# Differential attention in a two-block transformer kernel: scores two tiles ahead, three buffers per map, and a norm's passes moved within a tile

## The chip, the cores and the metric
The kernel runs on one core of one Trainium2 chip. The metric is device time in microseconds, the median of three runs: 2166.36 us before the change (2164.78 to 2167.35).

## What is computed
The reference runs a first transformer block (rotary attention, dilated attention, gates, a ReLU-squared MLP, a gated side input) and then a second one: a SwiGLU half step, a hybrid mixer of retention and differential attention, attention over a memory of 256 rows, and another SwiGLU half step. All is float32, on 512 tokens of 1024 features. The change is in the hybrid mixer's differential attention. This is the part that matters, cut:

```
def diff_attention(q, k, v, lam):          # 4 heads, 2 maps of 64, v of 128
    sc = einsum('bqhmd,bkhmd->bhmqk', q_blk, k) * scale
    sc = sc - slopes * dist                # ALiBi, causal
    p = softmax(sc, axis=-1)
    a = p[:, :, 0] - lam * p[:, :, 1]
    return einsum('bhqk,bkhe->bqhe', a, v)
do = rms_norm(do, diff_norm) * (1.0 - lam_init)
...
kv = (mem_n @ w_kv)                        # memory attention's keys and values
k = rms_norm(kv[:, :, 0], k_norm)
```

## The kernel before
Every engine's program is written out by hand, in order, and the engines meet at semaphores. Each linear layer is a chain of units: a unit multiplies one 1024 x 128 slice of weights (eight tiles) with the activations in three passes (high x high, high x low, low x high; L274 to L276 in `unit`), into one of two PSUM banks `acc`. GpSimd (`split_unit`) splits every slice of weights in a high and a low part, two units deep; SyncE's queue loads the slices six ahead.

The differential attention (`diff_pe`, `diff_act`, `diff_dve`) has 16 tiles: 4 heads by 4 blocks of 128 queries. Tile t = 4h + qt has 128 (qt + 1) keys, so the widths go 128, 256, 384, 512 and start again. Between its tiles TensorE does the memory attention's key and value projection, one unit a tile (`mem_unit`: tiles 0 to 7 the keys, 256 wide, 8 to 15 the values). A tile's steps are:
- TensorE: `score` (L1277), two matmuls into the PSUM banks `sc[0]` and `sc[1]`, one for each map. A bank is free when VectorE has read the tile before.
- VectorE: `d_scored_dve` (L1048), for each map, adds the ALiBi table, takes the row maximum and writes the buffer `p_d[m]`.
- ScalarE: `exp` (L1319) in that buffer, with the row sum read behind it.
- VectorE: `inverse` (L1404, L1406), the reciprocals of both sums.
- ScalarE: `inv` (L1326) scales map 0; VectorE: `combine` (L1414) adds map 1 to it.
- TensorE: `turn` (L1286), qt + 1 transposes into `tp`; ScalarE: `copy_pt` (L1332) copies them out. After a head's last tile `pv` (L1293) multiplies with V into `ob`.

Nine tiles also carry one norm (`DIFF_STAT`: tiles 2 and 3 the last head's q and k, 4, 5, 8, 9 the memory keys "mk0" to "mk3", 6, 10, 14 the outputs "do0" to "do2"; "do3" comes after the last tile). Such a norm is: a square on ScalarE (`k_sq` L1350, `o_sq` L1342), a sum over partitions on TensorE into the one PSUM bank `st` (`stat_pe`, L320), which waits for the square and for `stat_v`, four passes on ScalarE (`stat_act`, L330 to L337), the read of `st` on VectorE (`stat_v_dve`, L350), which raises `stat_v`, a Newton step (L357) and the product with the gain (L1034, L1420, L1428). `hr` and `vb` are single, so one norm's passes follow the other's. The order of the norms is fixed by `STATS`.

Before the change, TensorE's tile is: scores of tile t + 1, sums of the tile's norm, the unit, `pv` of the head before, the transposes. ScalarE's is: `inv(t)`, exponentials of t + 1, the four norm passes, copies, and the square for the next tile's norm at the end. VectorE's is: `inverse(t)`, maxima of t + 1, `combine(t)`, the copy of the unit's result, the norm's passes. There are two buffers for each map, so a maximum waits for the transposes two tiles back.

Outside the tiles: `ret_high_act` (L1097) and `ret_low_dve` (L1102) split the last retention head's result; `v_copy` (L1363) copies both banks of the memory values at tiles 11 and 15; `high` (L1367) and the end of `o_norm` (L1432) split a head's output for the output projection `mix_out_pe`, which follows.

## Time and profile before

| | us |
|---|---|
| median of three runs | 2166.36 |
| range of the runs | 2164.78 to 2167.35 |
| the profiled execution's own time | 2164.66 |
| its span | 2162.8 |
| TensorE busy in it | 2102.0 |
| the stage of the change, of the span | 94.0 |

The span runs from the first to the last instruction of the profiled execution; its own time is 1.9 us longer. PE is TensorE's matmuls, PEld its weight loads, DVE VectorE, ACT ScalarE, POOL GpSimd. Rows of the timeline give start, duration, engine, line, operation and operands, how many instructions a row merges, and in brackets the idle time before it and what ended that.

### The profile page before, as it was taken

The numbers are of one execution on the slowest core, as the hardware profiler recorded it, in microseconds if no ns is written. First come the engines' busy times: TensorE is split into PE (matmuls) and PEld (weight loads), VectorE is DVE, ScalarE is ACT, GpSimd is POOL, SyncE is SP. The second block draws the span as 40 slices with busy tenths as digits, with TensorE's granted clock in tenths as the row PEclk, the third lists the DMA queues.
The fourth block names the chain that finished last, engine by engine and source line by source line (L and its number), as shares of the span: only waits on it lengthen the run. The fifth ranks groups of instructions, "written<-read, shape, count | busy, mean of one in ns | idle before, by whom it ended". The sixth has DMA issues, their size and how long they took to land.

```text
span 2162.8 us, 29025 instructions
## 1 busy us (share of the span) xinstructions
PE 2102.0 (97%) x9198; PEld 1672.5 (77%) x9198; DVE 775.2 (36%) x1242; ACT 501.8 (23%) x911; POOL 1396.4 (65%) x1372
## 2 busy tenths in 40 slices
PE   7999999999999999989999999999899999999997
PEld 5878866678888888767888887877667778888885
DVE  4123344443320122282223126344765452221024
ACT  2023243331210121141110012134652421110011
POOL 5643333367777777667777779655667357777675
PEclk8999999999999999999999999999999999999998
DMA  7311111122222223222222224222222112222221
GB/s 247 114 58 39 49 49 49 49 78 97 97 97 97 97 96 105 92 78 88 97 97 98 97 97 165 91 74 69 88 78 98 59 59 97 97 97 97 97 97 58
DMA packets 55682, 193.84 MB, mean 90 GB/s; under 512 B 6303, under 2 KB 8607, under 8 KB 55236
## 3 DMA queue, kind: packets, MB, share of 16 engines
q1 hardware_dynamic: 51500, 184.05, 25.2%
q10 hardware_dynamic: 4120, 8.95, 1.2%
q8 instruction: 41, 0.67, 0.1%
q14 instruction: 21, 0.17, 0.0%
HBM read 190.85 MB, written 5.27 MB: 91 GB/s over the span
## 4 chain that ended last, share of the span: by engine, by line
PE 90%; DVE 5%; ACT 3%; issue 1%; DMA 0%; DVEq 0%; POOL 0%; SPq 0%; ACTq 0%; POOLq 0%
PE acc L274 26%; PE acc L276 26%; PE acc L275 26%; PE st L320 2%; PE ob L669 1%; PE sc L654 1%; PE ob L482 1%; DVE ssum L398 1%; PE sc L495 1%; PE sc L1500 1%; PE sc L497 1%; PE tp L662 1%; DVE arena L1619 0%; PE tp L528 0%; PE st L617 0%
## 5 line engine op out<-in xcount | busy, mean ns | idle before, releaser
L1705 POOL TENSOR_TENSOR w_lo<-w_raw,w_hi 128x512 fp32r<-128x512 f32 x684 | 927.4, 1356 | 57.1
L1703 POOL TENSOR_SCALAR w_hi<-w_raw 128x512 fp32r<-128x512 f32 x684 | 471.1, 689 | 689.1 <-PE acc L276 657.4
L274 PE MATMUL acc<-h_hi,w_hi 128*128 128x512 f32 x1936 | 779.6, 403 | 20.1 <-DVE h_lo L1838 8.6
L276 PE MATMUL acc<-h_hi,w_lo 128*128 128x512 f32 x1936 | 756.4, 391 | 0.0
L275 PE MATMUL acc<-h_lo,w_hi 128*128 128x512 f32 x1936 | 756.1, 391 | 0.0
L274 PEld LDWEIGHTS acc<-h_hi,w_hi 128*128 128x128 f32 x1936 | 365.5, 189 | 112.1 <-issue 26.1
L275 PEld LDWEIGHTS acc<-h_lo,w_hi 128*128 128x128 f32 x1936 | 365.7, 189 | 84.7 <-issue 10.6
L276 PEld LDWEIGHTS acc<-h_hi,w_lo 128*128 128x128 f32 x1936 | 365.1, 189 | 77.3
L274 PE MATMUL acc<-hid_hi,w_hi 128*128 128x512 f32 x608 | 236.9, 390 | 0.1
L276 PE MATMUL acc<-hid_hi,w_lo 128*128 128x512 f32 x608 | 236.6, 389 | 0.0
L275 PE MATMUL acc<-hid_lo,w_hi 128*128 128x512 f32 x608 | 236.5, 389 | 0.0
L274 PEld LDWEIGHTS acc<-hid_hi,w_hi 128*128 128x128 f32 x608 | 114.1, 188 | 24.6 <-POOL w_lo L1705 0.7
L276 PEld LDWEIGHTS acc<-hid_hi,w_lo 128*128 128x128 f32 x608 | 114.1, 188 | 23.9
L275 PEld LDWEIGHTS acc<-hid_lo,w_hi 128*128 128x128 f32 x608 | 114.1, 188 | 23.5
L436 DVE TENSOR_TENSOR arena<-acc,rstd 128x512 f32<-128x512 f32 x64 | 44.1, 690 | 188.0 <-PE acc L276 187.0
L941 ACT ACTIVATE tmp<-tmp 128x512 f32<-128x512 f32 x44 | 27.8, 632 | 341.6 <-DVE tmp L950 341.6
L952 DVE TENSOR_TENSOR tmp<-acc,rstd 128x512 f32<-128x512 f32 x44 | 30.4, 691 | 200.4 <-PE acc L276 200.4
L421 DVE SCALAR_TENSOR_TENSOR x<-acc,x 128x512 f32 x24 | 16.6, 692 | 221.1 <-PE acc L276 220.7
L944 ACT CAST hid_hi<-tmp 128x512 f32 x44 | 27.3, 621 | 238.2 <-DVE tmp L955 238.2
L385 ACT ACTIVATE h_hi<-x,gain (+1 forms) x40 | 29.0, 725 | 186.0 <-DVE x L412 158.3
L398 DVE TENSOR_TENSOR ssum<-ssum,sq 128x512 f32<-128x512 f32 x64 | 68.3, 1067 | 9.1 <-ACT sq L388 8.4
L842 ACT ACTIVATE sq<-tmp 128x512 f32<-128x512 f32 x32 | 20.2, 633 | 209.9 <-DVE tmp L851 209.9
(255 smaller groups left out, 1774.4 us busy)
## 6 DMA issues: line engine op xcount, KB each, us to landing
w_raw<-in_wstream SPq DMA_DIRECT2D x342, 512.0 KB, 3.5
x<-in_xT SPq DMA_DIRECT2D x4, 512.0 KB, 6.4
bias_skew<-bias_rows ACTq DMA_DIRECT2D x4, 512.0 KB, 7.4
out_y<-x SPq DMA_DIRECT2D x8, 256.0 KB, 2.2
arena<-bias_skew ACTq DMA_DIRECT2D x4, 257.5 KB, 3.8
bias_skew<-bias_rows ACTq DMA_DIRECT2D x4, 256.0 KB, 8.0
arena<-in_memT ACTq DMA_DIRECT2D x1, 1024.0 KB, 8.4
arena<-in_decay ACTq DMA_DIRECT2D x1, 1024.0 KB, 11.8
```

The lines of the kernel that those rows point to most:

```text
L274: nc.tensor.matmul(dst, w_hi[:, slot, k, :], xh[:, k, :], start=first, stop=False)
L275: nc.tensor.matmul(dst, w_hi[:, slot, k, :], xl[:, k, :], start=False, stop=False)
L276: done = nc.tensor.matmul(dst, w_lo[:, slot, k, :], xh[:, k, :], start=False, stop=last)
L320: m = nc.tensor.matmul(st[:, 0:width], ones if lhs is None else lhs, part, start=j == 0, stop=j == len(parts) - 1)
L385: nc.scalar.activation(hi[:, n, :], x[:, n, :], ACT.Identity, scale=gain[:, GAINS[gname] + n:GAINS[gname] + n + 1] if isinstance(n, int) e ...
L398: nc.vector.tensor_tensor(ssum[:], ssum[:], sq[:, b, :], ALU.add).then_inc(h_sum, 1)
L436: nc.vector.tensor_tensor(dst, acc[n % 2][:, 0:width], rstd[:] if r is None else r, ALU.mult).then_inc(acc_read, 1)
L941: nc.scalar.activation(tmp[:, 0, :], tmp[:, 0, :], ACT.Silu).then_inc(pair_silu, 1)
L944: nc.scalar.copy(hid_hi[:, bass.ds(i, 1), :], tmp[:, 2:3, :]).then_inc(hid_hi_done, 1)
L952: nc.vector.tensor_tensor(tmp[:, 1, :], acc[1], rstd[:], ALU.mult).then_inc(acc_read, 1)
L1703: nc.gpsimd.tensor_scalar(w_hi[:, slot, ks, :], w_raw[:, raw, ks, :], 1.0, 0.0, ALU.mult, ALU.add).then_inc(w_rounded, 1)
L1705: nc.gpsimd.tensor_tensor(w_lo[:, slot, ks, :], w_raw[:, raw, ks, :], w_hi[:, slot, ks, :].bitcast(F32), ALU.subtract).then_inc(w_split, 1)
```

## The change
TensorE computes scores two tiles ahead instead of one, and issues them behind the tile's unit instead of in front of it. Each map gets a third buffer (two of the retention's decay tables, which are dead by then), and VectorE's maxima wait for the transposes and `combine` three tiles back. A norm's sums move from in front of the unit to the tile's end; ScalarE's four passes for them open the next tile, and VectorE's close it. `inv` is done one tile ahead, `combine` opens VectorE's tile. `k_sq` moves from the end of the tile before its sums into the tile of its sums, behind the exponentials and behind `o_sq`, which moves in front of `copy_pt`; `high` and the last step of `o_norm` (now `o_low`) move to the first tile of the head after next. `ret_low_dve(3)` moves in front of tile 1's maxima. No instruction is added or removed.

```diff
-        p_d = [[a2(28), a2(29)], [a2(32), a2(31)]]
+        p_d = [[a2(28), a2(29), a2(dt0)], [a2(32), a2(31), a2(dt0 + 1)]]
...
-            dve.wait_ge(turned, TILES0["diff"] + 4 * h + qt - 1)
-            dve.wait_ge(s("d_a"), counted(4 * h + qt - 1))
-            nc.vector.tensor_tensor_reduce(p_d[m][(e // 2) % 2][:, 0:w], sc[m][:, 0:w], alibi_s[:, h, SEQ - w:SEQ], 1.0,
+            dve.wait_ge(turned, TILES0["diff"] + 4 * h + qt - 2)
+            dve.wait_ge(s("d_a"), counted(4 * h + qt - 2))
+            nc.vector.tensor_tensor_reduce(p_d[m][(e // 2) % 3][:, 0:w], sc[m][:, 0:w], alibi_s[:, h, SEQ - w:SEQ], 1.0,
...
             d_v_turn_pe(pe, 3)
+            score(0, 1, 0)
+            score(0, 1, 1)
             for tile in range(4 * QT):
                 h, qt = divmod(tile, QT)
-                if tile < 4 * QT - 1:
-                    score((tile + 1) // QT, (tile + 1) % QT, 0)
-                    score((tile + 1) // QT, (tile + 1) % QT, 1)
-                if tile in DIFF_STAT:
-                    diff_stat_pe(pe, tile)
                 mem_unit(pe, tile)
+                if tile < 4 * QT - 2:
+                    score((tile + 2) // QT, (tile + 2) % QT, 0)
+                    score((tile + 2) // QT, (tile + 2) % QT, 1)
                 if h and qt == 0:
                     pv(h - 1)
                 turn(h, qt)
+                if tile in DIFF_STAT:
+                    diff_stat_pe(pe, tile)
             pv(3)
...
             ret_high_act(act, 3)
+            exp(0, 1, 0)
+            exp(0, 1, 1)
+            inv(0, 0)
             for tile in range(4 * QT):
                 h, qt = divmod(tile, QT)
-                inv(h, qt)
+                if tile - 1 in DIFF_STAT:
+                    stat_of(tile - 1)
                 if tile < 4 * QT - 1:
-                    exp((tile + 1) // QT, (tile + 1) % QT, 0)
-                    exp((tile + 1) // QT, (tile + 1) % QT, 1)
-                if tile in DIFF_STAT:
-                    stat_of(tile)
+                    inv((tile + 1) // QT, (tile + 1) % QT)
+                if tile < 4 * QT - 2:
+                    exp((tile + 2) // QT, (tile + 2) % QT, 0)
+                    exp((tile + 2) // QT, (tile + 2) % QT, 1)
+                if h and qt == 1:
+                    o_sq(h - 1)
+                if tile in DIFF_STAT and DIFF_STAT[tile][:2] == "mk":
+                    k_sq(int(DIFF_STAT[tile][2]))
                 if h and qt == 0:
                     o_copy(h - 1)
                 if tile in (11, 15):
                     v_copy((tile - 11) // 4)
                 copy_pt(h, qt)
-                if tile + 1 in DIFF_STAT and DIFF_STAT[tile + 1][:2] == "mk":
-                    k_sq(int(DIFF_STAT[tile + 1][2]))
-                if h and qt == 1:
-                    o_sq(h - 1)
-                if h and qt == 3:
-                    high(h - 1)
+                if h and qt == 0 and h > 1:
+                    high(h - 2)
             o_copy(3)
+            high(2)
...
+            ret_low_dve(dve, 3)
+            d_scored_dve(dve, 0, 1, 0)
+            d_scored_dve(dve, 0, 1, 1)
+            inverse(0, 0)
             for tile in range(4 * QT):
                 h, qt = divmod(tile, QT)
-                inverse(h, qt)
+                combine(h, qt)
                 if tile < 4 * QT - 1:
-                    d_scored_dve(dve, (tile + 1) // QT, (tile + 1) % QT, 0)
-                    d_scored_dve(dve, (tile + 1) // QT, (tile + 1) % QT, 1)
-                combine(h, qt)
-                if tile == 0:
-                    ret_low_dve(dve, 3)
+                    inverse((tile + 1) // QT, (tile + 1) % QT)
                 if tile < 8:
                     dve.wait_ge(w_used, 2 * (U0["mem_k"] + tile + 1))
                     nc.vector.tensor_copy(mem_k[:, tile, :], acc[tile % 2][:, 0:MEM]).then_inc(acc_read, 1)
-                if tile in DIFF_STAT:
-                    name, j = DIFF_STAT[tile], int(DIFF_STAT[tile][2])
+                if tile < 4 * QT - 2:
+                    d_scored_dve(dve, (tile + 2) // QT, (tile + 2) % QT, 0)
+                    d_scored_dve(dve, (tile + 2) // QT, (tile + 2) % QT, 1)
+                if h > 1 and qt == 0:
+                    o_low(h - 2)
+                if tile - 1 in DIFF_STAT:
+                    name, j = DIFF_STAT[tile - 1], int(DIFF_STAT[tile - 1][2])
                     if name[:2] == "mk":
                         k_norm(j)
                     elif name[:2] == "do":
                         stat_v_dve(dve, name, 128)
+                        o_norm(j)
...
-                if h and qt == 3:
-                    o_norm(h - 1)
+            o_low(2)
             stat_v_dve(dve, "do3", 128)
             o_norm(3)
+            o_low(3)
```

VectorE at the start of the stage, before: behind the last step of the retention (L1181) come tile 0's reciprocals, tile 1's maxima (L1048, each with its row for `mx`), tile 0's `combine` and then `ret_low`.

```order
L1181 TENSOR_TENSOR tmp<-tmp,arena 128x512
L1404 RECIPROCAL rl<-lsum 128x2
L1406 TENSOR_SCALAR rl<-rl,lam_t 128x1
L1048 ISA arena,mx<-sc,btmp 128x256
L1048 ISA mx 128x1
L1048 ISA arena,mx<-sc,btmp 128x256
L1048 ISA mx 128x1
L1414 SCALAR_TENSOR_TENSOR arena<-arena,rl 128x128
L1102 TENSOR_TENSOR h_lo<-tmp,h_hi 128x512
```

The same place with the change (line numbers of the changed kernel):

```order
L1181 TENSOR_TENSOR tmp<-tmp,arena 128x512
L1102 TENSOR_TENSOR h_lo<-tmp,h_hi 128x512
L1048 ISA arena,mx<-sc,btmp 128x256
L1048 ISA mx 128x1
L1048 ISA arena,mx<-sc,btmp 128x256
L1048 ISA mx 128x1
L1411 RECIPROCAL rl<-lsum 128x2
L1413 TENSOR_SCALAR rl<-rl,lam_t 128x1
L1421 SCALAR_TENSOR_TENSOR arena<-arena,rl 128x128
```

`ret_low` went from the end of the piece to its head; the maxima and `combine` stand behind it.

ScalarE around the norm step of tile 5, before. The square of mk1 (L1350) ends tile 4, tile 5 begins behind it.

```order
L1350 ACTIVATE tmp<-arena 128x512
L1326 ACTIVATE arena<-arena,rl 128x256
L1319 ACTIVATE arena,lsum<-arena,mx 128x384 x2
L330 ACTIVATE hr<-st,gain 128x256
L332 ACTIVATE hr<-hr 128x256
L335 ACTIVATE vb<-hr 128x256
L337 ACTIVATE hr<-hr 128x256
L1332 COPY arena<-tp 128x2x128
```

With the change, tile 5 begins with the passes of tile 4's norm and ends with the copy of its transposes (L1334):

```order
L330 ACTIVATE hr<-st,gain 128x256
L332 ACTIVATE hr<-hr 128x256
L335 ACTIVATE vb<-hr 128x256
L337 ACTIVATE hr<-hr 128x256
L1328 ACTIVATE arena<-arena,rl 128x384
L1321 ACTIVATE arena,lsum<-arena,mx 128x512 x2
L1344 ACTIVATE sq<-tmp 128x512
L1352 ACTIVATE tmp<-arena 128x512
L1334 COPY arena<-tp 128x2x128
```

The square of mk1 is now L1352, in tile 5, behind the exponentials of tile 7 (L1321) and the square of head 0's output (L1344).

TensorE at the same tile, before: the first transposes of tile 4, the scores of tile 6, the sums of mk1, then tile 5's unit.

```order
L1286 MATMUL tp<-mat_a,arena 128x128
L1277 MATMUL sc<-arena 128x384 x2
L320 MATMUL st<-tmp,mat_a 128x256 x2
L274 MATMUL acc<-mem_hi,w_hi 128x256
L275 MATMUL acc<-mem_lo,w_hi 128x256
L276 MATMUL acc<-mem_hi,w_lo 128x256
```

With the change, from the last matmul of tile 5's unit to the first of tile 6's:

```order
L276 MATMUL acc<-mem_hi,w_lo 128x256
L1277 MATMUL sc<-arena 128x512 x2
L1286 MATMUL tp<-mat_a,arena 128x128 x2
L320 MATMUL st<-tmp,mat_a 128x256 x2
L274 MATMUL acc<-mem_hi,w_hi 128x256
L275 MATMUL acc<-mem_lo,w_hi 128x256
```

The sums of mk1 moved from in front of tile 5's unit to behind it, and the scores in front of them are those of tile 7.

## Rows read from the trace of the kernel before

**Rows 1.** The page, part 1: busy us, share of the span, instructions.
```profile
PE 2102.0 (97%) x9198; PEld 1672.5 (77%) x9198; DVE 775.2 (36%) x1242; ACT 501.8 (23%) x911; POOL 1396.4 (65%) x1372
```

**Rows 2.** Window of the stage: length, busy us PE, PEld, DVE, ACT, POOL, clock.
```profile
1512.88:1606.87 93.99, 83.84 (x456) 61.38 (x455) 67.04 (x160) 64.44 (x155) 67.15 (x65) 1.00 0.26 90
```

**Rows 3.** Waits around the stage, TensorE: total us, times, longest.
```profile
PE tp L1286 <- DVE arena L1414: 5.4, 5, 1.5
...
PE st L320 <- ACT tmp L1350: 3.1, 4, 1.4
...
PE ob L1293 <- ACT arena L1332: 0.7, 1, 0.7
...
PE st L320 <- DVE vb L350: 0.4, 1, 0.4
...
PE st L320 <- ACT sq L1342: 0.3, 1, 0.3
```

**Rows 4.** Timeline of VectorE, start of the stage.
```profile
1518.51 0.42 DVE L1048 CUSTOM_DVE_ANT_0 arena<-sc,btmp 128x256 f32<-128x256 f32 x1
...
1518.86 0.42 DVE L1048 CUSTOM_DVE_ANT_0 arena<-sc,btmp 128x256 f32<-128x256 f32 x1
...
1519.24 0.35 DVE L1414 SCALAR_TENSOR_TENSOR arena<-arena,rl 128x128 f32<-128x128 f32 x1
1519.51 1.10 DVE L1102 TENSOR_TENSOR h_lo<-tmp,h_hi 128x512 fp32r<-128x512 f32 x1
```

**Rows 5.** Timeline of ScalarE, start of the stage.
```profile
1518.29 0.62 ACT L1097 CAST h_hi<-tmp 128x512 fp32r<-128x512 f32 x1 [1.39 <-DVE tmp L1181]
...
1519.12 0.49 ACT L1319 ACTIVATE arena<-arena,mx 128x256 f32<-128x256 f32 x1
```

**Rows 6.** Timeline of TensorE, tiles 0 to 5 and 11.
```profile
1519.65 0.33 PE L1286 MATMUL tp<-mat_a,arena 128*128 128x128 f32 x1 [1.46 <-DVE arena L1414]
1519.91 0.92 PE L1277 MATMUL sc<-arena 64*128 64x384 f32 x4
1520.76 0.39 PE L274 MATMUL acc<-mem_hi,w_hi 128*128 128x256 f32 x1
...
1523.74 0.38 PE L1286 MATMUL tp<-mat_a,arena 128*128 128x128 f32 x2
1524.05 1.13 PE L1277 MATMUL sc<-arena 64*128 64x512 f32 x4
1525.11 1.12 PE L320 MATMUL st<-sq,mat_b 128*128 128x512 f32 x2
...
1538.18 1.10 PE L320 MATMUL st<-tmp,mat_a 128*128 128x256 f32 x4 [1.37 <-ACT tmp L1350]
...
1541.99 2.32 PE L1293 MATMUL ob<-arena 128*128 128x512 f32 x8
...
1584.30 0.66 PE L1286 MATMUL tp<-mat_a,arena 128*128 128x128 f32 x4
...
1585.52 0.50 PE L1256 MATMUL acc<-w_hi,mem_hi 128*128 128x512 f32 x1
```

**Rows 7.** Timeline of VectorE, tile 3's maximum of the first map.
```profile
1525.21 0.69 DVE L1048 CUSTOM_DVE_ANT_0 arena<-sc,btmp 128x512 f32<-128x512 f32 x1 [0.53 <-PE sc L1277]
```

**Rows 8.** Timeline of ScalarE, passes of tiles 2, 3, 11 and 13.
```profile
1527.37 0.67 ACT L330 ACTIVATE hr<-st,gain 128x512 f32<-128x512 f32 x1
...
1537.40 0.63 ACT L1350 ACTIVATE tmp<-arena 128x512 f32<-128x512 f32 x1
...
1584.23 1.07 ACT L1363 COPY arena<-acc 128x512 f32<-128x512 f32 x2 [0.21 <-PE acc L1258]
```

**Rows 9.** Timeline of TensorE, two long waits elsewhere.
```profile
963.48 0.80 PE L274 MATMUL acc<-h_hi,w_hi 128*128 128x512 f32 x1 [3.11 <-DVE h_lo L915]
...
2149.57 1.72 PE L320 MATMUL st<-ssum,mat_a 128*128 128x512 f32 x2 [2.74 <-DVE ssum L398]
```

**Rows 10.** Window behind the first of them, columns as in rows 2.
```profile
963.00:969.00 6.00, 5.52 (x9) 3.07 (x10) 2.74 (x5) 2.05 (x3) 1.88 (x2) 0.51 0.08 11
```

More of the change, by code:

```diff
@@ L1285, in turn @@
                 for kt in range(qt + 1):
-                    m = nc.tensor.transpose(tp[e % 2][:, kt * P:(kt + 1) * P], p_d[0][e % 2][:, kt * P:(kt + 1) * P], ident)
+                    m = nc.tensor.transpose(tp[e % 2][:, kt * P:(kt + 1) * P], p_d[0][e % 3][:, kt * P:(kt + 1) * P], ident)
                 m.then_inc(turned, 1)
@@ L1317, in exp @@
                 act.wait_ge(row_max, WIDE0["diff"] + e + 1)
-                p = p_d[m][(e // 2) % 2][:, 0:w]
+                p = p_d[m][(e // 2) % 3][:, 0:w]
                 nc.scalar.activation(p, p, ACT.Exp, bias=mx[:, e % 8:e % 8 + 1], scale=-1.0,
@@ L1324, in inv @@
                 act.wait_ge(row_inv, TILES0["diff"] + e // 2 + 1)
-                p0 = p_d[0][(e // 2) % 2][:, 0:(qt + 1) * P]
+                p0 = p_d[0][(e // 2) % 3][:, 0:(qt + 1) * P]
                 nc.scalar.activation(p0, p0, ACT.Identity, scale=rl[:, e % 8:e % 8 + 1]).then_inc(s("d_p0"), 1)
@@ L1410, in combine @@
                 k, w = e % 8, (qt + 1) * P
-                p0, p1 = p_d[0][(e // 2) % 2][:, 0:w], p_d[1][(e // 2) % 2][:, 0:w]
+                p0, p1 = p_d[0][(e // 2) % 3][:, 0:w], p_d[1][(e // 2) % 3][:, 0:w]
                 dve.wait_ge(s("d_p0"), e // 2 + 1)
@@ L1430, in o_norm, with o_low @@
                 dve.sem_inc(hr_used, 1)
+            def o_low(h):
                 dve.wait_ge(s("d_hi"), h + 1)
                 nc.vector.tensor_tensor(h2_lo[:, 4 + h, :], tmp[:, 1, :], h2_hi[:, 4 + h, :].bitcast(F32), ALU.subtract).then_inc(s("d_lo"), 1)
+            ret_low_dve(dve, 3)
+            d_scored_dve(dve, 0, 1, 0)
+            d_scored_dve(dve, 0, 1, 1)
+            inverse(0, 0)
             for tile in range(4 * QT):
                 h, qt = divmod(tile, QT)
-                inverse(h, qt)
+                combine(h, qt)
                 if tile < 4 * QT - 1:
-                    d_scored_dve(dve, (tile + 1) // QT, (tile + 1) % QT, 0)
-                    d_scored_dve(dve, (tile + 1) // QT, (tile + 1) % QT, 1)
-                combine(h, qt)
-                if tile == 0:
-                    ret_low_dve(dve, 3)
+                    inverse((tile + 1) // QT, (tile + 1) % QT)
                 if tile < 8:
```

## The prediction

> **What bounds the kernel now.** I read the page first. TensorE is busy for 2102.0 of 2162.8 us and no other engine is above 65% [rows 1], so a change counts only where it moves TensorE's waits. The change touches one stage, the differential attention from its first scores to the first matmul of the output projection. The window view gives it 94.0 us, with TensorE busy for 83.8 of them at a granted clock of 1.00 [rows 2]; ten are waiting. The waits view names them [rows 3]: 5.4 us in five waits where a tile's transposes stand in front of VectorE's `combine`; 3.1 + 0.4 + 0.3 us in six where the sums of a norm stand in front of ScalarE's squares or of VectorE's read of `st` before; 0.7 us before the last product with V. Those 9.9 us are all that can be won, and 0.2% of the time, about what a measurement of this kernel can tell from no change, is 4.3 us.
>
> **How I price it.** A wait ends where the last thing it needs ends, so I follow TensorE's new order from issue to issue with the durations of the trace. M(t) is tile t's unit of the memory projection, S its two score matmuls, T its transposes. From issue to issue S and T take 0.85 and 0.26 us at 384 and 128 wide, 1.06 and 0.31 at 512 and 256 [rows 6]. Both maps of a tile run side by side, so VectorE can start only behind S: S of tile 3 starts at 1524.05, VectorE at 1525.21, or 1.16 later [rows 6, 7]. From there two maxima on VectorE and two exponentials on ScalarE fill 2.16 us, until ScalarE takes its next pass at 1527.37 [rows 7, 8]. The profile draws a matmul's end about 0.1 us into the next issue, so a wait counted from issue to issue is about 0.1 longer than in rows 3.
>
> **What goes.** With scores two tiles ahead, `inv` and `combine` of a tile are done before M(t) ends, so the waits of T at tiles 3, 6 and 10 go: 5.4 less 1.46 at tile 0 [rows 6] and less 0.26 at tile 15 is 3.7 us. The six norm waits of the old places go too, 3.8 us. With 0.1 for each of the nine, **8.4 us go**. The wait at tile 15 does not: there ScalarE still copies both banks of V (1.07 us, rows 8), then the transposes, and the product waits as before. The third buffers cost no instruction.
>
> **What comes.**
> - Start. VectorE's `ret_low(3)` now stands in front of tile 1's maxima. It needs ScalarE's cast, 1518.29 to 1518.91 [rows 5], and takes 1.10 [rows 4], to 1520.0. Two maxima of 256, 0.35 apart [rows 4], end near 1520.75; the exponentials (0.49 and their reads, rows 5) near 1521.5; only then come `inv(0)` (some 0.4) and `combine(0)` (0.35, rows 4), and T(0) at 1522.3, M(1) at 1522.55 against 1520.76 [rows 6]: **+1.8**.
> - Tiles 5 and 9. The sums of mk1 and mk3 need `k_sq`, which on ScalarE now stands behind the exponentials of tile t+2 and behind `o_sq`; those need S(t+2), which is now issued behind M(t). From the end of M(t): 1.16 + 2.16, then 0.53 for `o_sq` (a 512-wide pass hands over so long after its start: half of 1.07 for two copies) and 0.63 for `k_sq` [rows 8], and 0.15 until TensorE starts (1537.40 + 0.63 to 1538.18, rows 6, 8): 4.63. TensorE has S and T to do, 1.37. It waits 3.26 us, twice: **+6.5**.
> - Tiles 4 and 8: the same with S of 384 and no `o_sq`, about 3.6, but the product with V covers 2.2 [rows 6], S and T 1.1: 0.3 each, **+0.6**.
> - Tiles 3, 6 and 10: the sums wait for VectorE's read of `st` before them, now behind two maxima. Tile 3: 0.72 to the start, 0.69 for two maxima of 256, 0.69 for the read (as the 512-wide row of rows 7), 0.05, against 1.22 for S and T (1584.30 to 1585.52, the same widths) [rows 6]: 0.9. At tiles 6 and 10 S is 128 wide and the read 256, which makes 0.5 each. **+1.9**.
> - M(12) needs `v_copy(0)`, which stood behind exponentials already done and now stands behind those of tile 13: 0.72, 0.35 and two exponentials with reads (1.1), 0.55 for the first bank [rows 8] make 2.8 against 1.2 [rows 6]: **+1.6**.
>
> Sum: 1.8 + 6.5 + 0.6 + 1.9 + 1.6 = 12.4 against 8.4, so **4.0 us longer**. VectorE's closing passes of a norm lie beside M(t+1), which takes 2.98 (1520.76 to 1523.74, rows 6), and so do ScalarE's; they cost nothing. If M(t+1) didn't cover them the next `combine` would be late, about a microsecond a tile. `o_low(h-2)` holds VectorE for `high` at tiles 8 and 12; what it delays is the next `combine`, wanted only after a whole M. POOL and the DMA queues issue the same work in the same order.
>
> **The clock.** The trace has two waits of this length at full clock: 3.11 us ending at 963.48 and 2.74 us ending at 2149.57 [rows 9]. The granted clock after the first was 0.51 for six microseconds [rows 10], the lower of the two levels, 1.2 GHz: 0.49 x 6 = 2.9 us of work. The stage itself, with no wait above 1.46, kept 1.00 [rows 2]. The second wait was followed by a matmul that took 1.72 us [rows 9] where the same pair of 512-wide matmuls takes 1.1 [rows 6], so 0.6 us was lost before the work ended. A fall costs 0.6 to 2.9 us; I take 1.9, nearer to the longer wait, and one fall for the two waits, since both earlier ones had short bursts or a stage's end beside them and mine have a full unit ahead: **+1.9**. The Trainium skill speaks against this change here: "TensorE: Matmul & The Clock Gate", section "Why this matters for your kernels", asks for no long idle gaps between bursts of matmuls, since the gate goes back to half rate. By it both new waits would fall, and the sum would be 4.0 + 2 x 2.9 = 9.8; by the stage's own row it would be 4.0.
>
> Together 4.0 + 1.9 = 5.9. The profiled execution took 2164.66, so 2170.6 against its own time. The runs' median is 2166.36, 1.7 above it; against that the forecast is **2172.3 us**.
>
> **Rivals.**
> - No fall: +4.0, 2170.4, at the edge of what can be told. For it: TensorE's waits of this stage, up to 1.46 us, left the clock at 1.00 [rows 2, 6]. Against: rows 9 and 10. Chance 0.18.
> - Both fall: +7.8 to +9.8, 2174.2 to 2176.2. For it: the waits are 3.26 us and both waits above 2.5 had a slower matmul behind them. Chance 0.22.
> - The new waits are half as long: were the first map's scores out half way through S and its maximum and exponential under way while TensorE still works, the waits at tiles 5 and 9 would be 1.6 us each, and the sum 4.0 - 3.3 = +0.7, 2167.1. Against: VectorE's start at 1.16 [rows 6, 7] is behind the whole S. Chance 0.16, with all that lies between this and no change.
> - Faster: the squares come in time. The place is tiles 4, 5, 8 and 9: were `k_sq` ready when T ends, 7.1 of the 12.4 us would not come, and the kernel would be 3.1 us faster; with the reads of `st` in time too, 5.0, 2161.4. It decides where the stretch from S's start to `k_sq`'s end is shorter than S, T and the product, 1.37 us at tiles 5 and 9. For it: the old waits on `combine` are real, and a deeper look-ahead removes them. Against: the stretch is 4.63 us, and the order shows `k_sq` behind three passes that start after S. Chance 0.10, which also takes in milder gains.
> - The forecast, one fall: chance 0.34.
>
> **The numbers.** Range: from the faster case's mild half, 2164.5, to both falling at their full price, 2176.5; this leaves out some 0.1 below and less than 0.1 above. Slower by over 0.2% is the forecast (0.34), both falling (0.22) and a third of "no fall" (0.06): 0.62. Within 0.2%: the rest of "no fall" (0.12), the half waits (0.16), a mild gain (0.02): 0.30. Faster: 0.08.
>
> **What would show it.** Right: TensorE's waits on `combine` only at tile 0; two waits of about 3.2 us before the sums on `tmp`, released by ScalarE's square; about 1.6 us before M(12) released by V's copy; the stage about 98 us, 100 with a fall; a granted clock under 1.00 behind tile 5 or 9. Wrong: the waits at tiles 5 and 9 under 1.5 us, or the first product with V earlier than before by more than 2 us, would break the main term. A stage of 98 us and a clock of 1.00 would leave the sum and take away the fall.

## The result, and the profile after

The changed kernel takes **2173.23 us**, the median of seven runs (2169.23 to 2176.58). The kernel before, run beside it, took 2166.3 (seven runs). The ratio is 1.0041, 95% interval 1.0029 to 1.0053: slower, by 0.41% or 8.9 us as the ratio has it and by 6.9 as the two medians do. The forecast was 2172.3 and slower; the direction and the number came out, and the terms behind the number only in part.

TensorE's waits in the stage, in the form of rows 3 (waits view of the changed kernel, TensorE: total us, times, longest):

```profile
PE st L320 <- ACT tmp L1352: 7.6, 3, 3.1
PE sc L1277 <- DVE mx L1048: 2.1, 1, 2.1
PE st L320 <- DVE vb L350: 1.8, 3, 0.9
PE acc L1256 <- POOL w_lo L1720: 1.6, 1, 1.6
PE ob L1293 <- ACT arena L1334: 1.2, 1, 1.2
PE tp L1286 <- DVE arena L1421: 0.6, 1, 0.6
```

The five waits for `combine` of [rows 3], 5.4 us, have shrunk to one of 0.6 at the start. In their place stand three waits of the norm sums for ScalarE's square, 7.6 us. Ten waits of 14.9 us stand against twelve of 9.9. Where each is (timeline of the changed kernel, TensorE, every wait of the stage but the last product's):

```profile
1521.23 1.25 PE L1277 MATMUL sc<-arena 64*128 64x384 f32 x4 [2.13 <-DVE mx L1048]
1523.04 0.33 PE L1286 MATMUL tp<-mat_a,arena 128*128 128x128 f32 x1 [0.55 <-DVE arena L1421]
1538.74 1.13 PE L320 MATMUL st<-sq,mat_b 128*128 128x512 f32 x2 [0.88 <-DVE vb L350]
1554.68 2.04 PE L320 MATMUL st<-tmp,mat_a 128*128 128x256 f32 x4 [3.10 <-ACT tmp L1352]
1561.45 1.12 PE L320 MATMUL st<-sq,mat_a 128*128 128x512 f32 x2 [0.46 <-DVE vb L350]
1574.13 1.10 PE L320 MATMUL st<-tmp,mat_a 128*128 128x256 f32 x4 [1.40 <-ACT tmp L1352]
1582.53 2.05 PE L320 MATMUL st<-tmp,mat_a 128*128 128x256 f32 x4 [3.10 <-ACT tmp L1352]
1590.55 1.12 PE L320 MATMUL st<-sq,mat_a 128*128 128x512 f32 x2 [0.46 <-DVE vb L350]
1597.28 0.47 PE L1256 MATMUL acc<-w_hi,mem_hi 128*128 128x512 f32 x1 [1.62 <-POOL w_lo L1720]
```

In order: scores of tile 2 and transposes of tile 0, sums at tile 3, at tiles 5, 6, 8, 9 and 10, and tile 12's unit. Two of these rows show more than a wait: the sums at tiles 5 and 9 take 2.04 and 2.05 where the same row takes 1.10 at tile 8. The granted clock had fallen. The windows view shows it, first for the stage, here counted from the sums of the retention's last norm to the first matmul of the last product, then for the six microseconds behind the waits at the start and at tiles 5, 8 and 9 (columns as in rows 2):

```profile
1512.83:1616.15 103.32, 88.26 (x449) 64.77 (x448) 59.43 (x159) 63.49 (x154) 64.06 (x64) 0.93 0.24 79
1521.23:1527.23 6.00, 5.45 (x27) 4.78 (x28) 3.28 (x15) 3.94 (x12) 2.69 (x4) 0.72 0.26 90
1554.68:1560.68 6.00, 6.00 (x34) 5.39 (x35) 1.27 (x5) 2.45 (x6) 1.77 (x2) 0.74 0.16 63
1574.13:1580.13 6.00, 5.30 (x22) 3.40 (x22) 2.42 (x7) 3.54 (x9) 3.18 (x4) 1.00 0.29 87
1582.53:1588.53 6.00, 6.00 (x14) 4.77 (x15) 0.72 (x3) 2.44 (x6) 1.15 (x2) 0.51 0.19 72
```

The same stretch of the kernel before:

```profile
1511.93:1604.69 92.76, 82.61 (x450) 60.19 (x448) 66.22 (x159) 63.82 (x154) 65.67 (x64) 1.00 0.26 88
```

The stage is 10.6 us longer in this execution. The waits explain 5.0 of it. From issue to issue each wait costs 0.1 more than it is drawn, and there are two fewer, so 0.2 goes off: 4.8. The clock explains 6 x (0.28 + 0.26 + 0.49) = 6.2. That makes 11.0. Three falls, then, where the forecast had one: behind tiles 5 and 9, and one at the start, behind a wait of 2.13 us.

Why the sums at tile 5 come late is the order of ScalarE (timeline of the changed kernel, ScalarE at tile 5):

```profile
1551.97 0.72 ACT L1321 ACTIVATE arena<-arena,mx 128x512 f32<-128x512 f32 x1 [2.31 <-DVE mx L1048]
...
1552.70 0.71 ACT L1321 ACTIVATE arena<-arena,mx 128x512 f32<-128x512 f32 x1
...
1553.40 0.61 ACT L1344 ACTIVATE sq<-tmp 128x512 f32<-128x512 f32 x1
1553.92 0.61 ACT L1352 ACTIVATE tmp<-arena 128x512 f32<-128x512 f32 x1
```

ScalarE stood idle for 2.31 us before two exponentials that nobody needs yet, and both squares stand behind them though their inputs were there: the first experiment runs them right behind `inv`, 3.8 us earlier.

### The profile page after: what moved, and what is told of

Same layout as the page of the kernel before. It is cut to its first block, busy times and chain, and to the rows that moved or that the text cites. A ratio compares the mean times of both kernels' runs of the same rounds, so it can differ in the third digit from the quotient of the medians.

```text
span 2173.6 us, 29024 instructions
## 1 busy us (share of the span) xinstructions
PE 2107.3 (97%) x9198; PEld 1677.8 (77%) x9198; DVE 764.2 (35%) x1242; ACT 501.2 (23%) x911; POOL 1393.7 (64%) x1372
## 4 chain that ended last, share of the span: by engine, by line
PE 91%; DVE 5%; ACT 2%; issue 1%; POOL 0%; DMA 0%; DVEq 0%; SPq 0%; ACTq 0%; POOLq 0%
PE acc L274 26%; PE acc L276 26%; PE acc L275 26%; PE st L320 2%; PE ob L669 1%; PE sc L654 1%; PE ob L482 1%; DVE ssum L398 1%; PE sc L495 1%; PE sc L1515 1%; PE sc L497 1%; PE tp L662 1%; DVE arena L1634 0%; PE st L617 0%; PE tp L528 0%
## 5 line engine op out<-in xcount | busy, mean ns | idle before, releaser
L275 PEld LDWEIGHTS acc<-h_lo,w_hi 128*128 128x128 f32 x1936 | 365.4, 189 | 84.9 <-issue 10.6
```

The costliest lines, as they stand in the source:

```text
L275: nc.tensor.matmul(dst, w_hi[:, slot, k, :], xl[:, k, :], start=False, stop=False)
```

## The experiments

All were timed against the kernel before on the same chip. The interval of a ratio is about 0.001 on either side, some 2 us, so the profile has to say where an edit of 2 us went, and the ratios only whether the sum of it is real. "Stage" is the stretch measured above, 92.8 us in the kernel before. Times before the stage differ by up to 4.6 us between executions and are left out by it.

### The squares in front of the exponentials

```diff
-                if tile < 4 * QT - 2:
-                    exp((tile + 2) // QT, (tile + 2) % QT, 0)
-                    exp((tile + 2) // QT, (tile + 2) % QT, 1)
                 if h and qt == 1:
                     o_sq(h - 1)
                 if tile in DIFF_STAT and DIFF_STAT[tile][:2] == "mk":
                     k_sq(int(DIFF_STAT[tile][2]))
+                if tile < 4 * QT - 2:
+                    exp((tile + 2) // QT, (tile + 2) % QT, 0)
+                    exp((tile + 2) // QT, (tile + 2) % QT, 1)
```

> The changed kernel with ScalarE's squares (o_sq, then k_sq) in front of the exponentials of tile t+2 instead of behind them. Theory 'queue order': the sums of mk1 and mk3 no longer wait for the exponentials but only for VectorE's read of st, which stands behind the two maxima: 1.16 + 1.24 + 0.42 + 0.05 less 1.37 for S and T makes 1.5 us in place of 3.1 at tiles 5 and 9, none in place of 1.4 at tile 8, and the granted clock stays at 1.00 behind tiles 5 and 9. Waits 4.7 us less, clock 3 to 4.5 us less: near 2165. Rival 'look-ahead': what costs is that scores run two tiles ahead with three buffers, wherever the squares stand: the waits before the sums stay near 3, and the time at 2173 within 2 us.

2164.11 us (11 runs) against 2164.56, ratio 1.0001 (0.9992 to 1.001). Stage 93.6. This one move gives back nearly all that the change had cost. The wait and the fall of the clock at the start are still in it (0.72 behind tile 2's scores). TensorE's timeline at tiles 5 and 9:

```profile
1549.24 1.13 PE L320 MATMUL st<-tmp,mat_a 128*128 128x256 f32 x4 [1.36 <-DVE vb L350]
...
1572.38 1.13 PE L320 MATMUL st<-tmp,mat_a 128*128 128x256 f32 x4 [1.36 <-DVE vb L350]
```

The waits fall from 3.10 to 1.36, and their name changes: with the square in time, the read of `st` on VectorE is what the sums wait for. The wait at tile 8 (1.40) is gone, and the clock behind tiles 5 and 9 is 1.00. The stage's 93.6 is 9.7 less than the changed kernel's profiled execution, of which 3.5 + 1.4 are these waits and 6 x (0.26 + 0.49) = 4.5 the two falls. The main term of the forecast is shown.

### Idle matmuls in the two long waits

```diff
                 turn(h, qt)
+                if tile in (5, 9):
+                    pe.wait_ge(turned_copy, TILES0["diff"] + tile)
+                    for _ in range(3):
+                        nc.tensor.matmul(tp[(tile + 1) % 2], ident, rstd[:], start=True, stop=True)
                 if tile in DIFF_STAT:
                     diff_stat_pe(pe, tile)
```

> The changed kernel with three idle matmuls (float32, 512 wide, identity times a table, into the bank of the next tile's transposes) on TensorE in front of the sums of tiles 5 and 9; their results are overwritten. They take some 2.6 us, inside the waits of 3.1. Theory 'the wait lowers the clock': the sums start when they did, but the granted clock behind tiles 5 and 9 is 1.00, so the stage is 3 to 4.5 us shorter than in the changed kernel and the median near 2169. Rival 'the slow matmuls behind the waits have another cause' (the weights' split, reads of the same memory): the sums of tile 5 and 9 still take 2.0 us instead of 1.1, and the time stays at 2173, or above it by what the matmuls add.

2171.77 us (6 runs), ratio 1.0033 (1.0021 to 1.0044); stage 99.3. The products write a free bank and are never read. The clock did what was expected: the sums take 1.10 again, and the window over tile 5 shows the full clock (windows of this kernel, tile 5 and behind the start):

```profile
1549.00:1560.00 11.00, 10.48 (x62) 7.47 (x62) 4.87 (x14) 6.50 (x15) 5.57 (x6) 1.00 0.16 54
1521.95:1527.95 6.00, 5.44 (x27) 4.78 (x28) 3.29 (x15) 3.95 (x12) 2.85 (x4) 0.72 0.27 90
```

The fall at the start stays. The runs show 1.7 us less than the changed kernel's ratio, where 4 had been expected; both lie inside the intervals. The stage is 4.0 us shorter than in the first profiled execution of the changed kernel and 1.0 than in the second (below), so nothing here prices a fall. And one execution with two filled waits is thin evidence: of eight unfilled waits of this length, counted below, two passed without a fall, and two in a row would do so by chance one time in sixteen (an estimate from that count). It agrees with the theory that the idle time lowers the clock, and the windows end the rival, since the slow sums and the low granted clock stand in the same rows.

### The third buffer alone

```diff
-        p_d = [[a2(28), a2(29)], [a2(32), a2(31)]]
+        p_d = [[a2(28), a2(29), a2(dt0)], [a2(32), a2(31), a2(dt0 + 1)]]
...
-            dve.wait_ge(turned, TILES0["diff"] + 4 * h + qt - 1)
-            dve.wait_ge(s("d_a"), counted(4 * h + qt - 1))
+            dve.wait_ge(turned, TILES0["diff"] + 4 * h + qt - 2)
+            dve.wait_ge(s("d_a"), counted(4 * h + qt - 2))
```

This is the kernel before with the buffers of the change and nothing else.

> The kernel before with the third buffer alone: three buffers per map and maxima that wait for transposes and combine three tiles back, every order as before. Theory 'queue order': the maxima did not wait for their buffer, since scores ran only one tile ahead, so nothing moves: 2166 within 0.2%, TensorE's waits of the stage 9.9 us within 0.5. Rival 'the buffer itself' (the address of the new buffers costs, or the buffer frees the chain): maxima or exponentials longer by over 0.05 us each, or the time more than 2 us away.

2165.63 us (12 runs), ratio 1.0001 (0.9992 to 1.001). Every wait of rows 3 is there again, five for `combine` of 5.5 us and four for the square of 3.1. No maximum had been waiting for a buffer; the buffers only allow the deeper order.

### The start as it was

```diff
             ret_high_act(act, 3)
+            inv(0, 0)
             exp(0, 1, 0)
             exp(0, 1, 1)
-            inv(0, 0)
...
-            ret_low_dve(dve, 3)
+            inverse(0, 0)
             d_scored_dve(dve, 0, 1, 0)
             d_scored_dve(dve, 0, 1, 1)
-            inverse(0, 0)
+            combine(0, 0)
+            ret_low_dve(dve, 3)
...
-                combine(h, qt)
+                if tile:
+                    combine(h, qt)
```

> The changed kernel with the start of the stage ordered as before the change: on VectorE inverse(0), tile 1's maxima, combine(0), then ret_low(3); on ScalarE inv(0) in front of tile 1's exponentials. Theory 'queue order': the scores of tile 2 wait some 1.2 us instead of 2.1, the transposes of tile 0 not at all instead of 0.55, M(1) starts about 1.5 us earlier, and without the longer wait the clock stays at 1.00 there, another 1.5 to 2: 3 us less, near 2170. Rival 'the first scores of tile 2 are bound by something else' (the exponentials of tile 1 in ScalarE's queue): the two waits stay at 2.7 us together, 2173.

2170.62 us (8 runs), ratio 1.0028 (1.0018 to 1.0038); stage 99.8. Timeline of TensorE at the start of this kernel, the only wait left there:

```profile
1520.21 1.25 PE L1277 MATMUL sc<-arena 64*128 64x384 f32 x4 [0.81 <-DVE mx L1048]
```

The clock behind it is 1.00, and the ratio is 2.8 us under the changed kernel's, as expected; the wait left is 0.8 and not 1.2. The waits of 3.10 at tiles 5 and 9 stay, and the clock behind them is 0.50 and 0.72. The three kernels further down that have this start keep 1.00 behind it too. So the fall at the start belongs to the order of the start, and not to the deeper look-ahead.

### V's copy in front of the exponentials

```diff
+                if tile in (11, 15):
+                    v_copy((tile - 11) // 4)
                 if tile < 4 * QT - 2:
                     exp((tile + 2) // QT, (tile + 2) % QT, 0)
                     exp((tile + 2) // QT, (tile + 2) % QT, 1)
...
-                if tile in (11, 15):
-                    v_copy((tile - 11) // 4)
```

> The changed kernel with one edit: at tiles 11 and 15 ScalarE copies V's banks in front of the exponentials of tile t+2. The theory (M(12) waits for V's copy, which stands behind exponentials it doesn't need): the wait of 1.62 us before tile 12's unit goes to under 0.4, and the stage becomes about 1.5 us shorter than the changed kernel's 103.3; the runs come out about 1.5 us under the changed kernel's, near 2171.5, a ratio to the kernel before near 1.003. The last product's wait of 1.2 stays or shrinks a little. The rival, as the waits view of the changed kernel names it (1.6 us, released by POOL's low part of the weights): V's copy is not the cause, the wait stays at 1.6 and the time doesn't move. The three falls of the clock stay under both.

2173.53 us (12 runs) against 2165.2, ratio 1.0033 (1.0023 to 1.0042); stage 100.1. In this kernel's timeline the wait before tile 12's unit goes from 1.62 to 0.59 and is named after the copy:

```profile
1593.45 0.47 PE L1256 MATMUL acc<-w_hi,mem_hi 128*128 128x512 f32 x1 [0.59 <-ACT arena L1365]
```

POOL's split, which the waits view of the changed kernel had named, was not touched by the edit. In this kernel the unit starts at 1593.45, inside a pass of that split (1593.20 to 1594.49). So the name in that view was wrong and the cause V's copy. In front of the copy stand the four passes of the norm and `inv`, which end about where it starts, at 1592.74; the 0.59 is what they leave, and the estimate of under 0.4 was too low. The stage is 3.2 us shorter than in the first profiled execution of the changed kernel, 1.0 by this wait and 1.6 because the clock stayed at 1.00 behind tile 5: two falls came where three had been expected. A gain of 1 us is below what the runs resolve.

### Scores in front of the unit

```diff
+                if 0 < tile < 4 * QT - 2:
+                    score((tile + 2) // QT, (tile + 2) % QT, 0)
+                    score((tile + 2) // QT, (tile + 2) % QT, 1)
                 mem_unit(pe, tile)
-                if tile < 4 * QT - 2:
+                if tile == 0:
                     score((tile + 2) // QT, (tile + 2) % QT, 0)
                     score((tile + 2) // QT, (tile + 2) % QT, 1)
```

VectorE's two maxima move in front of its copy of the unit's result in the same way.

> The changed kernel with the scores of tile t+2 issued in front of tile t's unit for tiles 1 to 13 (so still two tiles ahead), and VectorE's maxima in front of its copy of the unit's result. The theory (the waits come because scores, maxima, exponentials and squares all stand behind the unit): maxima and exponentials now run beside the unit of about 3 us, the waits at tiles 5 and 9 fall from 3.10 to 1.2 or less, those for the read of st (0.88, 0.46, 0.46) go, and the falls of the clock at tiles 5 and 9 with them; the start keeps its 2.1 + 0.55 and its fall. Stage about 95, runs near 2165.5, ratio 0.999 to 1.001. The rival (the look-ahead of two itself, with its third buffer, costs the time, by VectorE and ScalarE passes that come due too late whatever TensorE does first): waits of 2.5 us or more stay at tiles 5 and 9 and the time stays above 2170.

2165.78 us (12 runs), ratio 1.0 (0.9991 to 1.001); stage 93.2, the clock 0.55 in the six microseconds behind the start's wait, low until 1525.98, and 1.00 in the rest of the stage. Waits view of this kernel:

```profile
PE sc L1277 <- DVE mx L1048: 2.5, 2, 2.1
PE st L320 <- DVE vb L350: 1.9, 3, 0.7
PE st L320 <- ACT tmp L1355: 1.3, 3, 0.7
```

The long waits are gone with the look-ahead still two tiles deep, which ends the rival that the look-ahead itself was the cost. Waits for the read of `st` did not go: tile 3's is 0.68 for 0.88, tile 6's 0.52 for 0.46, and the sums at tile 5, which no longer wait for the square, wait 0.68 for the read; only tile 10's is gone. That part of the expectation was wrong.

### Four orders mended together

This is the squares first, the start as it was and V's copy first, as above, and VectorE's read of `st` in front of the maxima, with its old place in the closing passes left empty:

```diff
+                if tile - 1 in DIFF_STAT:
+                    name = DIFF_STAT[tile - 1]
+                    stat_v_dve(dve, name, {"m": 256, "d": 128 if name[1] == "o" else 64}[name[0]], MEM if name[0] == "m" else SEQ)
                 if tile < 4 * QT - 2:
                     d_scored_dve(dve, (tile + 2) // QT, (tile + 2) % QT, 0)
                     d_scored_dve(dve, (tile + 2) // QT, (tile + 2) % QT, 1)
```

> The changed kernel with four of its orders mended: the squares in front of the exponentials, the start as in the kernel before, V's copy in front of the exponentials, and VectorE's read of st in front of the maxima. The theory (the terms of the sum add up, and every one of them is a place in an order, not the two tiles of look-ahead): waits left are about 0.8 at the start, at most 0.5 at tiles 5 and 9 and 1.2 before the last product, no fall of the clock; a stage of 87 to 90 us against 92.8 before, and runs 3 to 6 us under the kernel before, ratio 0.997 to 0.999. The rival (the gain goes elsewhere, because VectorE's combine or its copy of the unit's result becomes late behind the read of st, or the weights' split on POOL bounds the units): new waits of 2 us or more in sum appear on combine, on the accumulator's banks or on POOL, and the ratio is 1.000 to 1.002.

**2156.86 us** (6 runs, 2154.03 to 2158.89) against 2165.2, ratio 0.996 (0.9947 to 0.9974). It beats both kernels, by 8.3 us the one before. Its waits and its stage (waits view, then the window):

```profile
PE acc L1256 <- ACT arena L1365: 1.6, 1, 1.6
PE ob L1293 <- ACT arena L1334: 1.2, 1, 1.2
PE sc L1277 <- DVE mx L1048: 0.8, 1, 0.8
...
PE st L320 <- ACT tmp L1352: 0.3, 1, 0.3
```

```profile
1510.40:1595.74 85.34, 81.38 (x449) 59.98 (x447) 62.23 (x159) 62.98 (x154) 65.22 (x64) 1.00 0.30 95
```

Four waits of 4.0 us are left of twelve of 9.9, and the clock is full throughout. By these waits the stage should be 6.7 shorter than before (5.9, and 0.1 for each of the eight fewer); it is 7.4. The runs gained 8.3, more than the 3 to 6 expected. The difference lies inside the interval (5.6 to 11.5), and no run here settles it.

One wait did not go: the 1.6 before tile 12's unit. The exponentials are no longer in front of V's copy, but ScalarE's four norm passes are, and they began late: ScalarE waited 1.58 us for VectorE's closing products of the norm before, which hold `hr`. The early read of `st` was only run together with the other three moves, so its own share is not shown.

### The four orders with the scores first

Against the four orders, TensorE's tile changes as below, and VectorE's maxima again move in front of its copy of the unit's result:

```diff
+                if 0 < tile < 4 * QT - 2:
+                    score((tile + 2) // QT, (tile + 2) % QT, 0)
+                    score((tile + 2) // QT, (tile + 2) % QT, 1)
                 mem_unit(pe, tile)
-                if tile < 4 * QT - 2:
+                if tile == 0:
```

> The four mended orders together with the scores of tile t+2 in front of tile t's unit (tiles 1 to 13). The theory (both remedies attack the same waits, at tiles 5 and 9): no more than 1 us better than the four alone, since little is left to win; stage 87 to 89 us, ratio 0.997 to 0.999, the waits at tiles 5 and 9 gone altogether. The rival (with the maxima first, VectorE's copy of the unit's result and combine come late and the accumulator's bank is freed late): waits of TensorE on the bank in front of units, 1 us or more in sum, and a time 1 us or more above that of the four alone.

2160.13 us (12 runs), ratio 0.9973 (0.9964 to 0.9982); stage 88.1, 2.8 more than with the four alone. The rival had the size right and the place wrong. No unit waits for its bank; the scores do, four times, 4.0 us in all:

```profile
PE sc L1277 <- DVE mx L1048: 4.0, 4, 1.3
```

The 0.8 at the start is one of them and was there with the four orders. Of the others, tile 1 waits 0.98, tiles 8 and 12 wait 0.87 and 1.33. Scores issued in front of the unit need the score banks a unit earlier, and VectorE has not read them: at tile 1 its maxima stand behind `ret_low` (1.10 us), at tiles 8 and 12 behind the read of `st`, which waited 0.89 us for ScalarE's passes, and these for VectorE's closing products of the norm before. Those products were also slower here (below). Two remedies for one wait are not twice as good.

### V's copy once more

```diff
+                if tile == 11:
+                    v_copy(0)
                 if tile - 1 in DIFF_STAT:
                     stat_of(tile - 1)
...
-                if tile in (11, 15):
-                    v_copy((tile - 11) // 4)
...
                 copy_pt(h, qt)
+                if tile == 15:
+                    v_copy(1)
```

> The four mended orders with V's two copies moved once more: at tile 11 in front of the norm's four passes and inv, at tile 15 behind the copy of the transposes. The theory: in the four orders the wait of 1.63 us before tile 12's unit stays because V's copy stands behind the four passes (0.69 + 3 x 0.63 us) that begin late; with nothing in front of it it can start 0.2 us after tile 11's unit ends, ends 1.1 later and is covered by scores and transposes (1.2 us), so the wait falls to 0.3 or less. Before the last product the copy of the transposes no longer waits for V's (1.05 us): 1.22 goes to about 0.7. Together a stage about 2 us shorter (83.4 against 85.3) and runs near 2155, ratio 0.995. The rival (the wait is POOL's split of the weights, or the maxima of tile 13, which come later with the norm's passes): the wait at tile 12 keeps more than 1 us, or a wait of the same size appears at tile 13, and the time stays at the four orders' 0.996 or above.

2158.01 us (5 runs, 2155.43 to 2158.46), ratio 0.9965 (0.9952 to 0.9979); stage 85.2 against 85.3. Both waits that were aimed at shrank, 1.63 to nothing and 1.22 to 0.68, and the time went into others (timeline of TensorE: the product of tile 12, tile 13's transposes and the last product):

```profile
1582.91 2.42 PE L1293 MATMUL ob<-arena 128*128 128x512 f32 x8 [0.34 <-ACT arena L1334]
...
1590.46 0.44 PE L1286 MATMUL tp<-mat_a,arena 128*128 128x128 f32 x2 [1.05 <-DVE arena L1423]
...
1598.72 2.42 PE L1293 MATMUL ob<-arena 128*128 128x512 f32 x8 [0.68 <-ACT arena L1334]
```

V's copy was the cause of its wait; but behind it VectorE was late too. At tile 13 its `combine` stands, as in the changed kernel, behind `o_low` (L1443), which waited 2.05 us for ScalarE's cast (VectorE's timeline, same place):

```profile
1588.54 1.12 DVE L1443 TENSOR_TENSOR h_lo<-tmp,h_hi 128x512 fp32r<-128x512 f32 x1 [2.05 <-ACT h_hi L1369]
1589.58 0.82 DVE L1423 SCALAR_TENSOR_TENSOR arena<-arena,rl 128x256 f32<-128x256 f32 x1
```

The expectation (a stage of 83.4 and 2155 us) missed. The rival was right in the half that counts: 1.05 us at tile 13, with 0.34 before the product and 0.19 before tile 14's scores, make 1.6, as much as the wait that went.

### The changed kernel again

No edit.

> The changed kernel itself once more, unedited, beside the others on one chip, so that the others can be compared with it. Expected as before: 2173 us (2171 to 2175), a ratio of 1.003 to 1.005, three falls of the clock (at the start of the stage, behind tiles 5 and 9) and the same waits: 2.13 + 0.55, 3.10, 3.10, 1.4, 1.6, 1.2. If the mean clock is not 0.987 to 0.990 again, or the falls come at other places, then they are a matter of the execution and not of the waits.

2173.0 us (5 runs) against 2164.25, ratio 1.0041 (1.0027 to 1.0054), as the first time. Windows of its profiled execution, the stage and then behind the start and tiles 5 and 9:

```profile
1508.96:1609.23 100.27, 85.31 (x449) 62.11 (x447) 60.13 (x159) 63.49 (x154) 64.58 (x64) 0.97 0.25 81
1517.37:1523.37 6.00, 5.75 (x31) 4.65 (x31) 3.28 (x15) 3.94 (x12) 2.48 (x4) 0.72 0.28 91
1550.38:1556.38 6.00, 5.54 (x38) 4.71 (x38) 2.65 (x11) 3.69 (x11) 3.14 (x4) 1.00 0.16 63
1576.78:1582.78 6.00, 6.00 (x23) 4.52 (x23) 1.01 (x6) 2.46 (x6) 1.88 (x3) 0.76 0.15 59
```

The waits are the same to 0.3 us, and the clock is not: tile 5 kept the full clock behind its 3.10 us. The waits (14.8 us as drawn, 4.7 more than before when counted from issue to issue) and 6 x (0.28 + 0.24) = 3.1 for two falls make 7.8 us; the stage is 7.5 longer than before. So the same account, waits and clock, closes to 0.4 us in both executions of the changed kernel.

## Why the prediction was right, and where it was not

The direction was right for the reason given: `combine`'s waits went, and longer ones came, because `k_sq` stands on ScalarE behind exponentials that need scores issued behind the unit. Taken step by step:

- **What goes, 8.4.** `combine`'s waits are down to the one at tile 0, as said. The old norm waits went too. Confirmed.
- **Tiles 5 and 9, 3.26 each.** Measured 3.10 as drawn, 3.2 from issue to issue, in all four executions that have them. The squares in front of the exponentials took them to 1.36. Confirmed, with a second bound close behind that the forecast had not named: VectorE's read of `st`.
- **Tiles 3, 6 and 10, 0.9 + 0.5 + 0.5.** Measured 0.88, 0.46, 0.46. Confirmed.
- **M(12), 1.6.** Measured 1.62, and 1.83 in the other execution. Confirmed, against the name in the waits view, by two of the edits: with V's copy in front of the exponentials the wait fell to 0.59, and with nothing in front of the copy it was gone. (The stretch in that sum adds up to 2.7, not 2.8.)
- **Start, 1.8.** In the forecast's own terms, M(1) starts 10.31 us behind the first instruction of the stage (1523.14) against 8.83 before: 1.5 in place of 1.8. The waits before tile 2's scores and tile 0's transposes are 2.13 + 0.55 (0.24 in the other execution) against 1.46, 1.0 to 1.3 longer with 0.1 for the extra wait. The order was right; the clock that falls behind it was not in the sum.
- **Tiles 4 and 8, 0.3 each.** Tile 4 waited for nothing, tile 8 for 1.40: 1.4 instead of 0.6. By the rows shown below VectorE's closing passes were not costless at tile 8. The forecast had them "beside M(t+1)" at no cost; two of them and the `combine` behind them took 3.5 us there, and the maxima began only at 1571.56, 2.2 us behind the scores' issue.
- **The sum of the waits.** Forecast +4.0, measured +4.8 and +4.7. The last product's wait is 1.2 as drawn, against 0.7 before, together with tile 15's 0.3 that it took over.
- **The clock, one fall of 1.9: the step that failed.** The profiled executions show 6.2 and 3.1 us lost. The reason given for one fall, that full units stand ahead of these waits, did not hold; nor did the rival that both fall each time. Four profiled executions of three kernels have the waits of 3.10 us, eight of them (the changed kernel twice, V's copy first, the start as it was). The clock in the six microseconds behind was 0.74 and 0.51, 1.00 and 0.76, 1.00 and 0.52, 0.50 and 0.72: six of eight fell, 1.7 us lost on average. And one place was missing altogether: the clock fell at the start in every execution that had the wait of 2.1 us there, six of six, at 1.7 us in five and 3.4 in the one with the scores first.

So a typical execution pays 4.8 for waits, 1.7 for the start and 2 x 1.7 behind tiles 5 and 9: 9.9, against a ratio that says 8.9 (6.3 to 11.5). The stage was forecast 4 us longer, 6 with the fall; it was 10.6 and 7.5 longer. The forecast of 5.9 for the whole is too small in the clock, and its 2172.3 met the measured 2173.2 by luck in part: it stood on a median of before of 2166.4, while the kernel before gave medians of 2164.6, 2165.2 and 2164.3 beside the experiments.

The forecast's rule of the Trainium skill, "TensorE: Matmul & The Clock Gate", section "Why this matters for your kernels", asks for no long idle gaps between bursts. The trace agrees in part: by it the clock would fall behind both waits each time, and it did behind six of eight; and it fell each time behind the start's 2.13 us too, a gap that the forecast had not counted as long.

## What to carry to other kernels

A deeper look-ahead moves the work that it advances in front of work that was due now; go through each engine's order and put what another engine is about to wait for ahead of what is needed a tile later. Here that was four short moves, and it turned 0.4% slower into 0.4% faster with the same instructions. When a wait is shortened, read who would release it next before counting its whole length as won: the squares' wait hid one for `st`, and V's copy hid one of VectorE.

## What the runs showed of the hardware

**The clock fell behind a wait of 2.1 us, each time.** In the six executions with the changed start TensorE waited 2.12 or 2.13 us before tile 2's scores. The granted clock in the six microseconds from their issue was 0.72 five times and 0.55 once, that is, it went to the lower level, 1.2 GHz, for part of them (the changed kernel: 0.50 from 1524.00 to 1527.00). The matmul rows behind show it: 256-wide matmuls took 0.41 in place of 0.28. The shorter wait that often follows is not what brings the fall. With V's copy first there was none, and the clock was 0.63 in the first half microsecond of the scores and 0.50 in the next, so that the same scores took 1.99 in place of 1.25 (timeline of TensorE in that kernel, scores of tile 2 and transposes of tile 0):

```profile
1520.60 1.99 PE L1277 MATMUL sc<-arena 64*128 64x384 f32 x4 [2.12 <-DVE mx L1048]
1522.53 0.47 PE L1286 MATMUL tp<-mat_a,arena 128*128 128x128 f32 x1
```

The four orders with the scores first had a pair, 0.81 and 0.98 us, and kept 1.00. Single waits of 1.3 to 1.8 us left the clock at 1.00 everywhere in this stage: the 1.84 before tile 12's unit is the longest. What tells the six falls of eight behind 3.10 us from the other two is open; the order of work around them was the same. Nor does a fall need a wait: in the kernel before, the clock was 0.59 from 207 to 211 us, though TensorE has no wait drawn between 195 and 212. No run here shows why.

**VectorE's passes from SBUF wait for GpSimd's.** The timeline of the changed kernel around tile 8, GpSimd's rows and then VectorE's:

```profile
1567.16 1.30 POOL L1720 TENSOR_TENSOR w_lo<-w_raw,w_hi 128x512 fp32r<-128x512 f32 x1
1568.43 1.06 POOL L1718 TENSOR_SCALAR w_hi<-w_raw 128x512 fp32r<-128x512 f32 x1
```

```profile
1566.79 0.69 DVE L350 SCALAR_TENSOR_TENSOR vb<-st,vb 128x512 f32<-128x512 f32 x1
1567.51 1.50 DVE L357 SCALAR_TENSOR_TENSOR hr<-vb,hr 128x512 f32<-128x512 f32 x1
1569.05 0.98 DVE L1435 SCALAR_TENSOR_TENSOR tmp<-tmp,gain,hr 128x512 f32<-128x512 f32 x1
1570.26 1.03 DVE L1421 SCALAR_TENSOR_TENSOR arena<-arena,rl 128x128 f32<-128x128 f32 x1 [0.24 <-DVE tmp L1435]
```

L357 began inside GpSimd's 1.30 us, which ended at 1568.46, and itself ended 0.55 later; with GpSimd idle it takes 0.69, and at 256 wide it took 0.43 at 1580.77 with GpSimd idle and 1.08 at 1590.53 beside it. GpSimd's next pass in turn took 1.06 where it takes 0.62 alone. L350, which reads a PSUM bank, kept its 0.69 beside GpSimd. `combine`, beside GpSimd too, took 1.03 where it took 0.35 in rows 4. L357, L1435 and L1421 together, 3.5 us, hold back the maxima, the exponentials and so the square that tile 8's sums wait for; that they account for the whole of 1.4 in place of 0.3 is a reading of these rows, and no run isolates it. The kernel before has the same: L357 took 1.75 there at 1584.16. The four orders with the scores first met the same more often; its closing products, beside those of the four orders alone (groups of VectorE's instructions in the stage, eight of them: busy us, mean ns):

```profile
L1430 DVE SCALAR_TENSOR_TENSOR arena<-arena,gain,hr 128x256 f32<-128x256 f32 x8 | 8.2, 1065 | 0.1
```

```profile
L1427 DVE SCALAR_TENSOR_TENSOR arena<-arena,gain,hr 128x256 f32<-128x256 f32 x8 | 5.7, 752 | 0.1
```

The Trainium skill, "SBUF — State Buffer", section "SBUF: two separate sides", says that VectorE and GpSimd share one pair of ports under an exclusive lock, which whoever starts first holds for the whole instruction, and names VectorE's operations with two SBUF inputs among those that take it, against an operation of GpSimd that reads SBUF. The trace agrees: 1.50 against 0.69 with GpSimd's pass first; and where L357 started first (1583.37 in the second execution of the changed kernel, 256 wide) it took 0.42 and GpSimd's pass 1.47 in place of 1.27.

**A name in the waits view can be another's.** The wait before tile 12's unit was put down to GpSimd's `w_lo` in one execution of the changed kernel (1.62) and to V's copy (L1365) in the other (1.83), with the same order of work; in the first, both ended within 0.2 us of the unit's start. The edits decide for V's copy.
